# Latent attention in a two-block transformer kernel: transposes alternate between two PSUM banks, scores between two in place of three

## The reference

```python
MLA_HEADS, QK_NOPE, QK_ROPE, V_HEAD, Q_BLOCK = 4, 128, 64, 128, 128

def causal_block_attention(q, k, v):          # q, k: 512 tokens x 4 heads x 192; v: x 128
    scale = Dqk ** -0.5
    def one_block(args):                      # 128 queries against all keys
        qblk, start = args
        s = jnp.einsum('bqhd,bkhd->bhqk', qblk, kf) * scale
        mask = kpos[None, :] <= qpos[:, None]
        s = jnp.where(mask[None, None], s, -jnp.inf)
        p = jax.nn.softmax(s, axis=-1)
        return jnp.einsum('bhqk,bkhd->bqhd', p, vf)
    out = lax.map(one_block, (qb, starts))
```

## Time and profile before

| | us |
|---|---|
| median of 3 runs | 1304.42 (1304.26 to 1304.53) |
| profiled execution, time | 1303.2 |
| its span, first to last instruction | 1301.9 |
| TensorE busy | 1290.2 (99% of the span) |
| VectorE busy | 883.2 (68%) |
| ScalarE busy | 723.2 (56%) |
| GpSimd busy | 790.9 (61%) |
| chain that ended last | PE 85%, DVE 7%, ACT 4%, POOL 3% of the span |

### The profile page before, as it was taken

How to read it: one execution, slowest core, us unless ns; L and a number is a source line. 1 busy time by engine, 2 the same in 40 slices (tenths; PEclk the granted TensorE clock), 3 DMA queues, 4 the chain that set the end, 5 groups by cost and what they waited for, 6 DMA issues and landing times.

```text
span 1301.9 us, 21566 instructions
## 1 busy us (share of the span) xinstructions
PE 1290.2 (99%) x8286; PEld 1125.3 (86%) x8286; DVE 883.2 (68%) x1520; ACT 723.2 (56%) x1339; POOL 790.9 (61%) x546
## 2 busy tenths in 40 slices
PE   9999999999999999999999999999999999999998
PEld 6787778879898898998788888776789999999998
DVE  5796694966265472642558574747589977987888
ACT  4532585476463363544655556645477655765664
POOL 3643425977376575665557363643377876887785
DMA  9685245333333233233422122111123332333233
GB/s 378 242 310 210 80 153 194 114 114 108 103 106 105 90 104 122 83 98 107 131 91 93 49 66 65 65 62 37 58 75 112 102 110 98 98 114 114 98 102 111
DMA packets 41831, 152.08 MB, mean 117 GB/s; under 512 B 4352, under 2 KB 5120, under 8 KB 40960
## 3 DMA queue, kind: packets, MB, share of 16 engines
q1 hardware_dynamic: 40848, 147.41, 32.9%
q0 software_dynamic: 448, 2.62, 0.5%
q10 hardware_dynamic: 432, 0.67, 0.1%
HBM read 147.80 MB, written 2.10 MB: 115 GB/s over the span
## 4 chain that ended last, share of the span: by engine, by line
PE 85%; DVE 7%; ACT 4%; POOL 3%; issue 1%; DVEq 0%; ACTq 0%; POOLq 0%
PE bank L837 23%; PE bank L839 23%; PE bank L838 23%; PE bank L1367 2%; POOL wL L3648 2%; PE bank L884 1%; PE bank L886 1%; PE bank L885 1%; PE bank L938 1%; POOL acc L3658 1%; DVE small L2826 1%; PE bank L931 1%; PE bank L898 1%; ACT wH L1735 1%; PE bank L923 1%
## 5 line engine op out<-in xcount | busy, mean ns | idle before, releaser
L3648 POOL TENSOR_TENSOR wL<-raw,wH 128x1024 fp32r<-128x1024 f32 (+1 forms) x115 | 284.9, 2485 | 255.3 <-ACT wH L1735 252.2
L837 PE MATMUL bank<-hH,wH 128*128 128x512 f32 (+1 forms) x544 | 210.4, 387 | 1.7 <-POOL wL L3648 0.6
L839 PE MATMUL bank<-hH,wL 128*128 128x512 f32 (+1 forms) x544 | 200.6, 369 | 0.0
L838 PE MATMUL bank<-hL,wH 128*128 128x512 f32 (+1 forms) x544 | 200.3, 368 | 0.0
L1735 ACT ACTIVATE wH<-raw 128x1024 fp32r<-128x1024 f32 (+1 forms) x115 | 120.6, 1050 | 93.5 <-PE bank L839 67.0
L3653 POOL TENSOR_TENSOR wL<-raw,wH 128x512 fp32r<-128x512 f32 (+1 forms) x96 | 122.6, 1278 | 53.7 <-ACT wH L1744 52.9
L837 PE MATMUL bank<-gH,wH 128*128 128x256 f32 x512 | 145.4, 284 | 0.3 <-POOL gL L3653 0.3
L839 PE MATMUL bank<-gH,wL 128*128 128x256 f32 x512 | 144.9, 283 | 0.0
L838 PE MATMUL bank<-gL,wH 128*128 128x256 f32 x512 | 144.9, 283 | 0.0
L837 PEld LDWEIGHTS bank<-hH,wH 128*128 128x128 f32 x544 | 102.8, 189 | 25.3 <-issue 6.5
L839 PEld LDWEIGHTS bank<-hH,wL 128*128 128x128 f32 x544 | 102.6, 189 | 18.0
(11 more groups left out here) (511 smaller groups left out, 3638.8 us busy)
## 6 DMA issues: line engine op xcount, KB each, us to landing
raw<-in_wall SPq DMA_DIRECT2D x211, 512.0 KB, 3.3
rows<-in_wall SPq DMA_DIRECT2D x24, 1024.0 KB, 11.2
bra<-in_rpbw SPq DMA_DIRECT2D x8, 360.0 KB, 4.6
xq<-in_xt SPq DMA_DIRECT2D x2, 1024.0 KB, 6.7
xT<-in_xn SPq DMA_DIRECT2D x1, 2048.0 KB, 7.9
out_x<-xT SPq DMA_DIRECT2D x6, 256.0 KB, 2.9
vE<-in_ctxt SPq DMA_DIRECT2D x1, 1024.0 KB, 20.7
icn<-in_invc POOLq DMA_DIRECT2D x1, 1024.0 KB, 8.9
```

What stands on the lines that cost most here:

```text
L837: matmul(o, a_h, b_h, start=first, stop=False)
L838: matmul(o, a_h, b_l, start=False, stop=False)
L839: return matmul(o, a_l, b_h, start=False, stop=last)
L3648: tt(wL[i % NHL][:, 0:n], raw[load(c) % NRAW][:, 0:n], wH[i % NHL][:, 0:n].bitcast(F32), ALU.subtract).then_inc(s.w_lo, 1)
```

## The change

One line of the table that describes the latent attention is edited. The scores alternate between banks 0 and 1, and the transposes between banks 2 and 6. The releases follow, since `scores` and `latent_pair` set `freed[sc(i)]` and `turn` sets `freed[pt(i)]`.

```diff
     memory = NA(16, MEM0, MEM1, lambda i: 256, lambda i: i % 2, lambda i: 2, lambda i: 3, P2, PT2, lambda i: qcol(0, i))
-    latent = NA(16, LAT0, LAT1, lambda i: 128 * (latent_head(i)[1] + 1), lambda i: (0, 1, 6)[i % 3], lambda i: 2,
+    latent = NA(16, LAT0, LAT1, lambda i: 128 * (latent_head(i)[1] + 1), lambda i: i % 2, lambda i: (2, 6)[i % 2],
                 lambda i: (3, 7)[i % 2], P3, PT3, latent_scale)
```

## The result

The changed kernel takes 1309.79 us in the median of 6 runs (1308.86 to 1310.88); the kernel before, 1304.25 (6 runs). The ratio is 1.0045, with a 95% interval of 1.0035 to 1.0055: 5.5 us slower. The forecast was 1309.3 us with 1306.2 to 1311.2 as its range. The profiled execution of the changed kernel took 1308.86 us with a span of 1307.6, 5.7 above the span before.

The account below looks back on a forecast made before the run. TensorE was taken to bound the kernel. For the profiled execution 1303.2 + 4.66 of delay + 0.2 for waits gave 1308.1 us; for the median 1304.4 + 4.9 = 1309.3 us, range 1306.2 to 1311.2.

Parts of the forecast that it names:

- The bound: Latent attention, 878 to 933 us: TensorE, busy 53.26 of 55.00 us, sets the end, so added waits aren't given back.
- Which steps wait: Score pairs: third product waits for VectorE's normalising at steps 2, 4, 6, 8 and 14, not at 10 and 12.
- The loop: TensorE and VectorE delay each other from pair to pair in the latent attention; delay reaches 4.98 us, ending at 4.66.
- delay D: Lateness of a score pair's third L1596 product, the first of score i+1: 1.50 us at step 2, 4.98 at 14.
- What a wait costs beside its length: Extra TensorE time at each of five waits in score pairs: 0 to 0.1 us each, 0.2 taken in all.
- The transposes' gain: Odd steps: transposes stop waiting for ScalarE's copy, about 1.5 us in all; 0.21 at step 9, 0.32 at 15 stay.
- (a): Score pairs: VectorE early at every step, no pair waits, transposes' gain kept whole, 1302.9 us; chance 4%.
- (b): Score pairs: bank released late, but half the wait is hidden, 1306.4 us; chance 10%.
- (c): Latent attention: TensorE's clock falls to 1.2 GHz after one gap, up to 7 us longer, 1316 us; chance 3%.
- longer dense pieces: Sign of being wrong: TensorE's dense pieces, 12 products each at even steps of the latent attention, grow longer; no size given.
- (d): Score pairs: signals or restarts cost 0.3 us more over five pairs, or ScalarE's copy precedes more exponentials; 1311.4 us, chance 8%.
- The rule on banks: Rotating matmul groups through PSUM banks: promises transposes about -1.5 us, speaks against taking a scores' bank; the second outweighs.

Follow-up runs that it names:

- the halves apart: Kernel before with only the scores put on two banks, transposes left on bank 2: stage 6.04 us longer, against 5.50 for the full change; median 6.5 us above.
- transposes_two_only: Kernel before with scores kept on three banks, transposes of odd items put in the bank their own score just left: 1302.83 us, ratio 0.9990.
- two_where_late: Kernel before with scores reusing the two last banks at steps 2 and 4 alone, transposes in bank 2: 1307.66 us, ratio 1.0029.
- after_again: The changed kernel run once more, unaltered, against the kernel before, to look at its clock: 1309.59 us, ratio 1.0045.

## Why the prediction was right, step by step

**The bound.** Right. TensorE is as busy behind the stage as before, and the 5.50 us of the stage are the whole change.

**Which steps wait.** Right at all seven. The near miss at step 12 (0.3 us of lead) held for the product. It was near indeed: the sixth wait in the row of PEld is there, where the weight load of the third product waited 0.24 us for VectorE and the product itself not at all.

**The loop.** The delay D of the third product, less the 0.13 us by which the stage began later in the profiled execution:

| step | predicted | measured |
|---|---|---|
| 2 | 1.50 | 1.50 |
| 4 | 3.45 | 3.62 |
| 6 | 3.68 | 4.01 |
| 8 | 4.87 | 5.35 |
| 14 | 4.98 | 5.62 |
| end of the stage | 4.66 | 5.50 |

The error grows by 0.1 to 0.2 with each wait behind the first, and by nothing between waits. That is the next point.

**What a wait costs beside its length.** This is the term that was mis-sized. I bounded it at 0 to 0.1 us a wait, took 0.2 in all, and had only the short products of the earlier trace rows to read it from. Measured, from the third product to L1599: 881.44 - 880.81 = 0.63 us where the earlier trace rows give 0.475 at that width, and 889.42 - 888.58 = 0.84 for 0.69. That is 0.15 us at each. The other three waits show it too: 1.06 and 1.05 us for 0.905 at width 512, 0.42 for 0.27 at 128. Five times 0.15 is 0.8. With it the sum is 4.66 + 0.8 = 5.4, and 5.50 was measured. The fault was in the reading of the earlier trace rows: the 0.1 there is a difference of two durations, and the durations differ by no more here (0.70 for 0.59, 0.91 for 0.81, 0.49 for 0.38). What moves the work behind is the time from one start to the next, and that grew by 0.15. The forecast of the change was 4.9 us and 5.5 came; this term is the difference.

**The transposes' gain.** Right in kind and, for the changed kernel, in size: no L931 waits, and the halves apart differ by 6.04 - 5.50 = 0.54 us, where 0.21 + 0.32 was the gain to be kept. The gain with three banks for the scores was put at about 1.5, from six waits of 0.2 to 0.3 us. That estimate was a misreading: the weight loads of L931 wait 0.56, 0.54, 0.32 and 0.44 us at steps 3, 5, 7 and 13. And yet only 1.1 was won: from pair to pair transposes_two_only is 0.18 to 0.25 us shorter around each of steps 5, 7, 9, 13 and 15, and no shorter around step 3 (5.45 for 5.44 us). The length of a wait only bounds what its removal gives.

**The rivals.** That VectorE is early at every step (a) is refuted by the five waits. That half is hidden (b) is refuted as well: the waits come through in full, and two_where_late gives nothing back. The clock (c) was given 3% and a price of up to 7 us. It is partly true: it falls in 4 of 11 executions, and 1.1 us lie between the medians of the two kinds. I reasoned from 150 to 200 us, where TensorE idles 2.15 us in small pieces at clock 1.00. Here the gap before the fall was 1.40 us in one piece, with 0.35 more behind it. But the length of the gaps doesn't decide it: the profiled execution of the changed kernel has the same two, 1.39 and 0.35, and one of 1.84 behind them, and no fall. What decides stays open. One sign of being wrong that I had named, longer dense pieces, did show in such executions: 0.63 us for 0.39 a product in after_again, and not in the profiled execution of the changed kernel. A longer loop (d) is the restart above, at half the price that I gave it.

**The rule on banks.** Both sides of it showed, each in its own kernel: rotating the transposes won 1.1 us, taking a bank out of the scores' rotation lost 6.0. The Trainium skill, Perfetto Trace Analysis, section Matmuls under Optimizing Tensor Performance, asks for such a rotation; transposes_two_only keeps it for both.

## What to carry to other kernels

How many banks a ring needs follows from the step at which the next user claims against the step at which the last one is released. Here the pair claims at step i what VectorE releases in step i, and the release is there in time at two of seven pairs. Read for each claim when it would come and when the release comes, and then follow the delay around the loop, for the engine that releases is itself fed by what is waiting. And before a stage's buffers are shared out anew, look for one that has just been freed by the operation's own input: the bank of score j was free for the transposes of j, and the scores kept their three banks.

## What was not expected of the hardware

A wait on TensorE cost 0.15 us beyond its length before fp32 products of 128 to 512 columns: 0.42 us for 0.27, 0.63 for 0.475, 0.84 for 0.69, 1.06 for 0.905. TensorE's clock fell to 1.2 GHz after a gap of 1.40 us and a second of 0.35, and after one of 2.09, and stayed at 1.00 after 1.39, 0.35 and 1.84 in another execution of the same kernel. A clock that falls between two waits for another engine can cost nothing: 1.7 us of TensorE's work were taken out of a wait that would have been 1.5 us longer.
